# One broadcast product per adaptation tile on GpSimd, sixteen tiles instead of twelve, and other steps for the sums

## What is computed

```python
x = x + 0.5 * swiglu(rms_norm(x, ffn1_norm[l]), ffn1_gate[l], ffn1_up[l], ffn1_down[l])
...
x = x + mix @ w_out[l]
x = x + 0.5 * swiglu(rms_norm(x, ffn2_norm[l]), ffn2_gate[l], ffn2_up[l], ffn2_down[l])
```

```python
m = jax.nn.silu(cvec) @ w + b          # w_ada: 1024 x 6144 in each of two layers
```

## Time and profile before

| | us |
|---|---|
| median of 3 runs | 1927.23 (1926.27 to 1930.47) |
| the profiled execution | 1931.64 |
| its span in the trace | 1929.8 |
| PE busy | 1886.5 (98%) |
| DVE busy | 1282.9 (66%) |
| ACT busy | 917.9 (48%) |
| POOL busy | 248.1 (13%) |

### The profile page before, as it was taken

How to read it: one execution, slowest core, us unless ns; L and a number is a source line. 1 busy time by engine, 2 the same in 40 slices (tenths; PEclk the granted TensorE clock), 3 DMA queues, 4 the chain that set the end, 5 groups by cost and what they waited for, 6 DMA issues and landing times.

```text
span 1929.8 us, 28502 instructions
## 1 busy us (share of the span) xinstructions
PE 1886.5 (98%) x11774; PEld 1619.5 (84%) x11774; DVE 1282.9 (66%) x1666; ACT 917.9 (48%) x1289; POOL 248.1 (13%) x174
## 2 busy tenths in 40 slices
PE   7999999999999999999999999999999999979998
PEld 6888978888888888788889878988888889679997
DVE  5776796777677768777664464765554357857774
ACT  5334565334533455643454355543343345755553
POOL 0000007841756600000000110000000000000000
PEclk9999999999999999899999999999999999999999
DMA  7775436776567642776452221323223223024452
GB/s 279 264 265 215 175 119 256 275 268 232 204 241 287 235 168 95 271 263 253 153 187 108 109 78 66 110 88 104 104 87 109 88 88 120 24 88 175 175 196 88
DMA packets 50960, 323.78 MB, mean 168 GB/s; under 512 B 5472, under 2 KB 9744, under 8 KB 12816
## 3 DMA queue, kind: packets, MB, share of 16 engines
q1 hardware_dynamic: 39024, 270.09, 38.6%
q10 hardware_dynamic: 10080, 39.28, 5.3%
q0 software_dynamic: 1728, 12.58, 1.7%
HBM read 320.86 MB, written 1.07 MB: 167 GB/s over the span
## 4 chain that ended last, share of the span: by engine, by line
PE 79%; DVE 13%; ACT 5%; issue 2%; DMA 0%; ACTq 0%; DVEq 0%
PE ps L558 76%; DVE s_wl L1938 4%; DVE s_tmp L2037 3%; ACT s_wh L1267 3%; DVE s_xx L1938 2%; PE ps L911 1%; DVE s_tmp L2055 1%; DVE s_big L2237 1%; PE ps L768 0%; PE ps L745 0%; ACT s_big L1437 0%; PE ps L873 0%; DVE s_big L2060 0%; DVE s_tmp L2459 0%; DMA s_X<-in_x 0%
## 5 line engine op out<-in xcount | busy, mean ns | idle before, releaser
L558 PE MATMUL ps<-s_xx,s_wh 128*128 128x512 f32 (+1 forms) x3328 | 896.7, 347 | 11.9 <-DVE s_wl L2008 10.6
L1938 DVE TENSOR_TENSOR s_wl<-s_raw,s_wh 128x2048 fp32r<-128x2048 f32 x213 | 494.2, 2322 | 287.5 <-ACT s_wh L1267 287.5
L558 PE MATMUL ps<-s_xx,s_wl 128*128 128x256 f32 (+1 forms) x2208 | 669.1, 303 | 0.5 <-DVE s_xx L2462 0.5
L558 PEld LDWEIGHTS ps<-s_xx,s_wh 128*128 128x128 f32 x3328 | 579.7, 190 | 99.9 <-DVE s_wl L2008 10.9
L1267 ACT ACTIVATE s_wh<-s_raw 128x2048 fp32r<-128x2048 f32 x213 | 403.9, 1906 | 114.2 <-PE ps L558 110.0
L558 PEld LDWEIGHTS ps<-s_xx,s_wl 128*128 128x128 f32 x2208 | 419.3, 190 | 19.2 <-issue 2.7
L558 PE MATMUL ps<-s_wh,s_hl 128*128 128x512 f32 (+1 forms) x608 | 232.1, 382 | 2.4 <-DVE s_tmp L2037 1.9
L558 PE MATMUL ps<-s_wh,s_hh 128*128 128x512 f32 (+1 forms) x608 | 230.1, 378 | 0.0
L558 PE MATMUL ps<-s_wl,s_hh 128*128 128x512 f32 (+1 forms) x608 | 229.9, 378 | 0.0
L558 PE MATMUL ps<-s_wh,s_xx 128*128 128x256 f32 x928 | 179.2, 287 | 0.0
L1381 ACT ACTIVATE s_tmp<-s_tmp 128x512 f32<-128x512 f32 x44 | 27.8, 632 | 299.4 <-DVE s_tmp L2055 299.4
(11 more groups left out here) (238 smaller groups left out, 1849.3 us busy)
## 6 DMA issues: line engine op xcount, KB each, us to landing
s_raw<-in_ffn_down SPq DMA_DIRECT2D x44, 1024.0 KB, 4.8
s_raw<-in_w_up SPq DMA_DIRECT2D x44, 1024.0 KB, 4.7
s_raw<-in_ffn_gate SPq DMA_DIRECT2D x43, 1024.0 KB, 4.9
s_raw<-in_ffn_up SPq DMA_DIRECT2D x43, 1024.0 KB, 4.8
s_big<-in_w_ada ACTq DMA_DIRECT2D x34, 1024.0 KB, 6.7
s_raw<-in_w_down SPq DMA_DIRECT2D x22, 1024.0 KB, 4.7
s_raw<-in_w_in SPq DMA_DIRECT2D x18, 1024.0 KB, 4.8
s_X<-in_w_ada POOLq DMA_DIRECT2D x12, 1024.0 KB, 6.9
```

The costliest lines, as they stand in the source:

```text
L558: return pe.matmul(o, lhsT, rhs, start=start, stop=stop, skip_group_check=True)
L1938: dve.tensor_tensor(wide(wl, u), raw[:, u % SLOTS, :].rearrange("p (k n) -> p k n", k=8), f32(wide(wh, u)), SUB).then_inc(*w_low.tick(u))
```

## The change

Sixteen tiles go to POOL (32 to 47) in place of twelve (36 to 47), and PE does 32 fills in place of 36; the four fills that go are those behind j = 1 and j = 3 of ffn2 in layer 1. On POOL the eight products by a column become one product of the whole tile (2048 columns) with the condition vector's eight columns, each broadcast over 256 columns; the folds stay, and the wait that each of the first two folds had on its own pieces becomes one wait for the product. The row sums are read behind j = 5 and j = 10 of ffn2 in layer 0 and behind j = 2 and j = 8 of ffn1 in layer 1; before they were in down step 2 of ffn2 in layer 0, behind j = 4 and in down step 7 of ffn1 in layer 1. The third group of fills holds eight tiles in place of twelve, and the turn into columns has 8 and 4 in place of 12 and 3 where it counts tiles and sums.

```diff
--- before.py
+++ after.py
@@ -67,10 +67,10 @@
 
 
 ADA_AT = {("ffn1", 0): {2: 1, 4: 2, 6: 2, 8: 2}, ("ffn2", 0): {1: 2, 4: 2, 7: 2}, ("ffn1", 1): {1: 1, 4: 2, 7: 2},
-          ("ffn2", 1): {1: 2, 3: 2, 5: 2, 7: 2}}
+          ("ffn2", 1): {5: 2, 7: 2}}
 SUMS_AT = {("ffn1", 0): {},
-           ("ffn2", 0): {13: 36},
-           ("ffn1", 1): {4: 40, 18: 44}, ("ffn2", 1): {}}
+           ("ffn2", 0): {5: 32, 10: 36},
+           ("ffn1", 1): {2: 40, 8: 44}, ("ffn2", 1): {}}
 
 
 def weight_order():
@@ -647,13 +647,13 @@
 
                 pe.wait_ge(*half[g])
                 pe.wait_ge(*picked[0])
-                n = 12
+                n = 8 if g == 2 else 12
                 for c in range(2):
                     o = ps[7][:, 48 * g:48 * g + 4 * n].rearrange("p (f c s) -> p f c s", c=2, s=2)[:, :, c, :]
                     m = mm(o, tmp[:, 5, 128 * c:128 * c + 128], pick[:, 0:2 * n].rearrange("p (f s) -> p f s", s=2), True,
                            True)
                 if g == 1:
-                    a, n = 36, 3
+                    a, n = 32, 4
                     row = const("ident").rearrange("p (i j) -> p j i", i=4)[:, 24:24 + n, :]
                     for c in range(2):
                         o = ps[7][:, 4 * a:4 * a + 16 * n].rearrange("p (v i c s) -> p v i c s", i=4, c=2, s=2)[:, :, :, c, :]
@@ -675,7 +675,7 @@
                 w = ada_buf(f).rearrange("p (k n) -> p k n", k=8)
                 for k in range(8):
                     rows = slice(32 * (k % 4), 32 * (k % 4) + 32)
-                    m = mm(ps[7][rows, 256:512], c_strip(k, i), w[:, k, :], i == 0 and k < 4, i == 11 and k >= 4)
+                    m = mm(ps[7][rows, 256:512], c_strip(k, i), w[:, k, :], i == 0 and k < 4, f in (11, 23, 31) and k >= 4)
                 m.then_inc(*product.tick(("fill", f)))
 
             def row_sums(a):
@@ -683,7 +683,7 @@
                 pe.wait_ge(*cleared["ones"])
                 pe.wait_ge(*rows_summed[a + 3])
                 for i in range(4):
-                    m = mm(ps[7][32 * i:32 * i + 32, 256:512], ones_strip((a - 36) // 4), row_sum(a + i),
+                    m = mm(ps[7][32 * i:32 * i + 32, 256:512], ones_strip((a - 32) // 4), row_sum(a + i),
                            False, False)
                 m.then_inc(*product.tick(("row sums", a + 3)))
 
@@ -1284,9 +1284,9 @@
                 f = fills[0]
                 fills[0] += 1
                 act.wait_ge(*product["fill", f])
-                if f + 2 < 36:
+                if f + 2 < 32:
                     act.dma_start(ada_buf(f), a["w_ada"][f + 2]).then_inc(*ada_in[f % 2].tick(f + 2))
-                if f % 12 == 11:
+                if f in (11, 23, 31):
                     g = f // 12
                     if g:
                         act.wait_ge(*product["columns", g - 1])
@@ -2771,17 +2771,16 @@
                 load_rows(fs[0])
                 for f in fs:
                     pool.wait_ge(*rows_in[f])
-                    for k in range(8):
-                        pool.tensor_scalar(rows[:, k, :], rows[:, k, :], strip_c[:, k, 0:1], None, MUL).then_inc(
-                            *multiplied.tick((f, k)))
+                    pool.tensor_tensor(rows, rows, strip_c[:, :, 0:1].to_broadcast([128, 8, 256]), MUL).then_inc(
+                        *multiplied.tick(f))
+                    pool.wait_ge(*multiplied[f])
                     for k in (0, 4):
-                        pool.wait_ge(*multiplied[f, k + 3])
                         pool.tensor_tensor(rows[:, k:k + 2, :], rows[:, k:k + 2, :], rows[:, k + 2:k + 4, :], ADD).then_inc(
                             *folded.tick((f, k)))
                     pool.wait_ge(*folded[f, 4])
                     pool.tensor_tensor(rows[:, 0:2, :], rows[:, 0:2, :], rows[:, 4:6, :], ADD).then_inc(*folded.tick((f, 8)))
                     pool.wait_ge(*folded[f, 8])
-                    if f >= 40:
+                    if f >= 36:
                         pool.wait_ge(*product["row sums", f // 4 * 4 - 1])
                     pool.tensor_tensor(row_sum(f), rows[:, 0, :], rows[:, 1, :], ADD).then_inc(*rows_summed.tick(f))
                     if f < fs[-1]:
@@ -2800,7 +2799,7 @@
                 pool.memset(U[:, :, 0:16], 0.0).then_inc(*cleared.tick(("u", l)))
                 if l == 0:
                     pool.wait_ge(*product[("mix", 0), "t", 7, 1])
-                    sum_rows(range(36, 48))
+                    sum_rows(range(32, 48))
 
             pool.wait_ge(*cleared["u", 1])
             pool.wait_ge(*cb_in["two"])
```

## The result

The changed kernel takes 1965.66 us (median of 4 runs, 1963.81 to 1967.35), the kernel before 1927.32 beside it (4 runs, 1926.27 to 1930.47): a ratio of 1.0185, interval 1.0171 to 1.0200. The profiled execution of after is its fastest, 1963.81 us with a span of 1961.9; that of before was 1931.64. So the two traces differ by 32 us, the medians by 38.

What follows compares the result with a forecast made beforehand. PE was taken to bound the kernel, with the DVE and ACT loop setting the pace in two gate and up stretches. Product 34.7 + folds 4.8 - 3.4 (fills, net) = + 36 us: median 1963, profiled execution 1968, range 1925 to 1982.

Steps and rivals of the forecast that it cites:

- The mechanism: Gate and up of ffn2 layer 0 and ffn1 layer 1: POOL's product holds DVE, lengthening the kernel; chance 0.75.
- The product's term: Gate and up of both stretches: 10.5 products delay DVE 3.3 us each, 34.7 us together; bounds 18 and 54.
- The estimate of 3.3: DVE's loop: delay in us per product, weighted by where it becomes ready; bounds 2.0 and 4.5.
- The down product: Down product of ffn2 in layer 0: tiles 41 to 43 fall there, covered by PE's longer steps, priced at nothing.
- a fallback: Down product, tiles 41 to 43: 1 us each if PE's cover is too thin.
- The folds: Gate and up: 6.5 tiles in place of 3.5 in ffn2, + 4.8 us; in ffn1 nothing.
- The fills: ffn2 of layer 1: four fills fewer on PE give 3.8 us.
- PE's wait at the steps: Behind j = 10 of ffn2: 4.6 us if nothing slows PE, but none with products and folds lengthening PE's side.
- the product that lets DVE pass: Rival: the product doesn't hold DVE and POOL comes late behind j = 10; 1928 us, no difference; chance 0.10.
- the faster case in which long operations give way: Rival: long operations yield to DVE as column products do, PE never waits; 1923.5 us; chance 0.12 for faster.
- the product at the columns' price: Rival: the product takes 7.3 us and holds DVE as long, delay near 6 us each; 1989 us; chance 0.03.
- the faster case, in which columns hold DVE all along: Rival: column products held DVE already, so no more hold, and PE never waits; 1923.5 us; chance 0.12 for faster.

Runs made afterwards that it cites:

- product_alone: Kernel before with only the eight column products exchanged for one broadcast product; twelve tiles, all fills and old steps kept: 1950.38 us, ratio 1.0102.
- no_product: Changed kernel without any product on POOL, the tiles summed unmultiplied: 1931.88 us, ratio 1.0011.
- product_twice: Changed kernel with every broadcast product done twice in a row: 1999.46 us, ratio 1.0356.
- the pieces: Changed kernel with the broadcast product cut into two, four or eight: 1952.94, 1947.24 and 1951.85 us.
- steps_late: Changed kernel with row sums read behind j = 6 and in down step 7 (ffn2), behind j = 5 and in down step 7 (ffn1): 1973.64 us.
- columns_no_folds: Changed kernel with the eight column products of before and the three folds on POOL left out: median 1926.83 us, ratio 1.0002.
- tiles_same_steps: Changed kernel with only the product undone: eight column products, sixteen tiles, 32 fills, the new steps: 1983.41 us, ratio 1.0287.
- tiles_alone: Changed kernel with the eight column products of before and row sums at later steps; sixteen tiles, 32 fills: 1944.37 us, ratio 1.0077.
- eight_pieces_late: Changed kernel with the product cut into eight pieces of 256 columns and row sums at later steps: 1942.11 us, ratio 1.0062.

## Why the prediction was right, and where it was off

**The mechanism** is the forecast one. DVE is held by the new product, in the two stretches in which DVE and ACT set the pace, and what DVE loses there the kernel loses. Shown by exchange (product_alone), by dose (no_product, after, product_twice) and by size (the pieces). The length of the first stretch follows the hold us for us: from before to steps_late, after and product_twice the hold grows by 20.8, 22.0 and 40.9 and the length by 19.7, 19.9 and 39.1. (In the second stretch the length grows by 0.9 to 2.5 us more than the hold.) Below before it ends: columns_no_folds has 5.9 us less hold in the first stretch and is only 0.5 us shorter there.

**Cover.** DVE's busy time grew by 48.8 us and the holds of the two stretches by 22.0 + 8.7 = 30.7; the remaining 18 us lie in the out projection and the down products, and of them the kernel felt no more than what the first down product grew by, 5.6.

**The product's term was over-sized**, 34.7 us against 27.3. Its eleven products in the two stretches hold 3.43, 2.04, 2.87, 2.04, 1.76, 3.43 and 3.42, then 0, 2.50, 3.43 and 2.39 us, 2.5 on average; 10.5 were forecast, at 3.3. The count was right, the delay 0.8 us too large, and the input that was off is the product's duration: 4.53 us by the slope between two sizes of adds, 3.62 measured. This product goes by another slope: 0.60, 1.03, 1.89 and 3.62 us are 1.68 ns a column where the adds gave 2.12. Whether that is the broadcast operand, the multiplication or the place of the operands isn't shown; no run has a product of two plain tensors. The estimate of 3.3 came from where in DVE's loop a product gets in; with 0.9 us less of product it would have been 2.4. (The 4497 ns of the Trainium skill, GPSIMD Engine Reference, section 3.1, for an add of this size, would have missed in the same way.)

**The down product was priced at nothing** and cost 5.6 us. The text had a fallback, 1 us for each of three products if the cover is too thin; the cover was too thin, and 3 us would still have been 2.6 short, as PE's clock fell too. The product at 462.67 belongs to the first stretch: it is the last of its seven and holds the subtraction L2030 at 464.11 for 3.43 us, which is part of what PE waits 11.46 us for. In the down product the one at 479.00 holds the split of 479.60, a fold behind it holds the next subtraction, and PE waits for that. Timeline of after, POOL, DVE and PE, then six windows of PE:

```profile
479.00 4.18 POOL L2774 TENSOR_TENSOR s_X<-s_X,s_big 128x2048 f32<-128x2048 f32 x1 [4.61 <-DMA s_X<-in_w_ada]
479.60 5.72 DVE L1938 TENSOR_TENSOR s_wl<-s_raw,s_wh 128x2048 fp32r<-128x2048 f32 x1
...
485.25 1.75 DVE L2030 TENSOR_TENSOR s_hl<-s_big,s_hh 128x512 fp32r<-128x512 f32 x1
...
487.15 0.47 PE L558 MATMUL ps<-s_wh,s_hl 128*128 128x512 f32 x1 [2.90 <-DVE s_hl L2030]
```

```profile
460.00:471.00 11.00, 0.00 (x0) 0.71 0.66 260
471.00:474.00 3.00, 2.55 (x6) 0.50 0.00 0
474.00:478.00 4.00, 4.00 (x17) 0.88 0.69 240
478.00:482.00 4.00, 4.00 (x19) 1.00 0.81 285
...
488.00:489.00 1.00, 1.00 (x5) 0.80 0.97 410
489.00:492.00 3.00, 3.00 (x9) 0.50 0.36 101
```

After 11.46 us in which PE did nothing the granted clock is 0.50, the 1.2 GHz level, until about 475 (the 0.88 of the third window is a mean of both levels): 2.55 x 0.50 + 4 x 0.12 = 1.8 us. Behind the wait of 2.90 us it falls once more, 1.4 us after PE has started again: 0.20 + 3 x 0.50 = 1.7 us. With the wait that is 6.4 us; 0.7 go off, as four row sums that before has in this down product now stand in gate and up, which leaves 5.7 for 5.6 measured. No term of the sum was for the clock.

**The folds** came to + 3.0 in the first stretch (22.0 less the 19.0 of products) and + 0.4 in the second; + 4.8 and 0 were forecast. **The fills** gave 4.0 us for 3.8.

**PE's wait at the steps**: none, as forecast. POOL's last sum for the step behind j = 10 starts at 456.43, the row sums on PE at 459.35; tiles came every 16 to 21 us, 20.4 were forecast. From its held sum at 398.73 to the end of that last one POOL took 58.4 us where 63.3 were forecast; PE takes 58.7 for the same steps without holds, so they would be about level. tiles_same_steps shows the wait that slower tiles bring.

**The total.** Against its own profiled execution the forecast was 1968 and the trace 1963.8, 4 us under it; against the median 1963 and 1965.7. In the traces: product and folds + 30.6 for + 39.5, down product + 5.6 for 0, the rest - 4.1 for - 3.4. The product was priced too dear and the down product at nothing; the two errors offset each other, so that the medians lie within 3 us is in part luck. Of the rivals, the product that lets DVE pass fell with product_alone (and with it the faster case in which long operations give way), the product at the columns' price with its row of 3.62 us, and the faster case, in which columns hold DVE all along, with columns_no_folds.

**Open.** Why pieces of the same total work hold DVE less is read from the sums and the stretched pieces; how the two engines take turns between them isn't shown. Sixteen tiles with columns and steps late enough for them were not found: at 23 to 33 us a tile POOL was late for the steps of both runs that tried. Why PE's clock fell behind a wait of 2.03 us in after and not behind one of 2.02 in tiles_alone isn't shown.

## What to carry to other kernels

The time that GpSimd saved here was paid by VectorE, which the new instruction keeps out. So price a cheaper GpSimd operation by its kind (a scalar per partition or a second tensor) and its length, at the place where it runs, and not by the time that it saves GpSimd. Where two engines already wait for one another in a loop, such a hold counts in full once the slack of PE's next step is used up, and behind a longer wait PE may run a while at half clock on top. If the long two-tensor operation has to be there, cutting it into pieces recovers part of the loss (+ 17 in place of + 38 with four), and the fewer of them fall into the tight stretches the better.

## What the runs showed of the hardware

- A GpSimd product with two tensors holds DVE's two-tensor instructions for nearly its whole length, up to 3.43 of 3.62 us. A product by a scalar per partition holds them for practically nothing: 1.4 us over two stretches, with 128 of them in the kernel.
- The product with a broadcast operand took less than an add, 1.03 against 1.28 us at 512 columns and 0.60 against 0.735 at 256.
- Behind waits of PE of 4.9, 4.8, 6.8 and 11.5 us (eight_pieces_late twice, tiles_alone, after) PE ran at a granted clock of 0.50 for 3.5 to 6 us and then at 1.00. By the share missing that is 1.8 to 3.0 us, beside the wait itself. In after the same is seen behind waits of 2.0, 2.3, 2.5 and 2.9 us (0.50 in 629 to 631, 680 to 683, 373 to 375 and 489 to 492); in tiles_alone the clock stayed at 1.00 behind one of 2.0.
